# Order of the small matmuls in the state-space stage: pair by pair, or one 32-channel slice after the other

## The chip, the cores and the metric

The kernel runs on one core of one Trainium2 chip. The number that is compared is the device time of one execution in microseconds (us), median of three runs. A core has five engines that run their own instruction lists and meet through semaphores: PE (TensorE, matmuls), DVE (VectorE), ACT (ScalarE), POOL (GpSimd) and SP (which here only issues the loads of the weights).

## The reference, cut to what matters

Two layers of a hybrid attention block are followed by one block whose second half of channels goes through a complex diagonal state-space model. Only that part is touched:

```
bu_re = einsum('blgc,gnc->blgn', u32, bb_re)      # 64 groups of 16 channels, 64 states each
bu_im = einsum('blgc,gnc->blgn', u32, bb_im)
_, _, s_re, s_im = lax.associative_scan(_scan_combine, (a_re_t, a_im_t, bu_re, bu_im), axis=1)
y = (einsum('blgn,gcn->blgc', s_re, c_re) - einsum('blgn,gcn->blgc', s_im, c_im)
     + d_skip.reshape(N_SSM_GROUPS, SSM_GROUP) * u32)
g = gelu(y)
```

The sequence has 512 tokens. The kernel takes them two at a time, so that a scan runs over 256 chunks (`CHUNKS`); for the two tokens of a chunk there are separate small matrices.

## The kernel before, in words

Everything that is large is a product of activations [128 x 512] with weights that are streamed from HBM in units of 4 x 256 columns. ACT rounds a unit to `w_hi` (line 532), POOL makes the rest `w_lo` (line 519), and PE multiplies three times (lines 1658 to 1660): 24 matmuls of 512 columns a unit. ACT may round a unit only when PE has finished the unit four places before it, since there are four slots. SP orders the loads in the order of the units.

The state-space stage has 16 steps (`STEPS`). Step m works on 64 channels, as two slices of 32 channels (half `h` = 0 and 1), each with 128 states:

- `inputs_step(m)` on PE: for each half and for the real and the imaginary part `r`, two float32 matmuls with 32 rows of weights and 128 columns of weights, [32*128] in the trace, over 256 chunks. The results stand in `s_ps` (m even) or `t_ps` (m odd, which the trace calls to_ps). They are counted on `bu_done`.
- `state_step(m)` on DVE: rotates them by an angle (lines 1456 to 1464), scans them (line 1471), rotates back (lines 1477 to 1486) and writes `s_re` and `s_im`. Line 1477 may overwrite `s_re` only when PE has used the states of the step before (`ssm_y`).
- `outputs_step(m)` on PE: for each half one matmul with 32 rows and 32 columns of weights ([32*32], line 2044) and four with 128 rows and 32 columns ([128*32], lines 2046 to 2052) into `o_ps`. They are counted on `ssm_y`.
- `gelu(k)` on DVE (lines 1493 to 1496) after every second step, then a tanh on ACT (line 770), then `gelu_end(k)` (line 1501).
- `trig(m + 1)` on ACT (lines 765 and 766) makes the sine and cosine of the next step from angles that DVE makes (lines 1433 to 1445).

The order is written out by hand. PE's list has 16 rounds. Round m has one or two units of gate weights (one in rounds 4, 8 and 12, two in the other rounds from 1 to 15), `inputs_step(m + 1)` behind the first of them, and `outputs_step(m - 1)` at the end. DVE's list for round m is `angles(m + 1)`, in every second round `gelu` and `gelu_end`, and `state_step(m)`. ACT's list for round m is the rounding of the units up to four places beyond those of round m, in some rounds a copy of gate values (line 779), `trig(m + 1)`, and in every second round the tanh. After the last step ACT issues the transfer that brings all gates back (line 805, att<-gate_scratch); DVE scales them (line 1559) and goes on.

A row tile or column tile below means that a matmul takes only 32 or 64 of the 128 rows or columns of PE's array, by the partitions of its operands; two such matmuls can use different parts of the array.

Of the kernel before, what the change touches and what calls it, by code (L numbers as in the profile page):

```python
# [178 lines left out]
def build_program(nc, x, positions, w_in, w_uq, w_ukv, w_out, p_2, w_in_2, w_pool_2, w_glu_2, w_out_2, w_ple_2,  # L179
                  w_ple_gate_2, params, ssm_params, consts, out):  # L180
    at, UNITS, ROUNDS = plan_units()
    with ExitStack() as ctx:
# [341 lines left out]
        def _(act):  # L524
# [279 lines left out]
            act.wait_ge(ssm_y, 2 * STEPS)  # L804
# [91 lines left out]
        def _(dve):  # L896
# [550 lines left out]
            def state_step(n):  # L1447
# [7 lines left out]
                dve.wait_ge(bu_done, 2 * n + 2)  # L1455
# [18 lines left out]
                if n:  # L1474
                    dve.wait_ge(ssm_y, 2 * n)
# [13 lines left out]
            def gelu(k):  # L1489

                y = tiles[:, 8 + k]
                dve.wait_ge(ssm_y, 4 * k + 4)
                own.link(stt(y, y, C("dskip", k), o_ps[:, k % 2, :], ALU.mult, ALU.add))
                own.link(tt(tmp_s, y, y, ALU.mult))
                own.link(ts(tmp_s, tmp_s, 0.044715, 1.0, ALU.mult, ALU.add))
                tt(tmp_s, tmp_s, y, ALU.mult).then_inc(gelu_in, 1)
# [155 lines left out]
        def _(pe):  # L1652
# [356 lines left out]
            def inputs_step(m):  # L2009
# [10 lines left out]
                chs = [slice(32 * q, 32 * q + 32) for q in (2 * (m % 2), 2 * (m % 2) + 1)]  # L2020
                for r in range(2):
                    ps = [(s_ps, t_ps)[m % 2][:, h, r * CHUNKS:(r + 1) * CHUNKS] for h in range(2)]
                    for h, ch in enumerate(chs):
                        pe.matmul(ps[h], b_st[ch, k, r], x_k[ch, 1], start=True, stop=False)
                    for h, ch in enumerate(chs):
                        mm = pe.matmul(ps[h], ab_st[ch, k, r], x_k[ch, 0], start=False, stop=True)
                        if r == 1:
                            mm.then_inc(bu_done, 1)

            def outputs_step(m):  # L2030
# [6 lines left out]
                half = []  # L2037
                for h in range(2):
# [3 lines left out]
                    half.append((ch, y, s_re[:, h * CHUNKS:(h + 1) * CHUNKS], s_im[:, h * CHUNKS:(h + 1) * CHUNKS]))  # L2042
                for ch, y, re, im in half:
                    pe.matmul(y[:, 0], cb_st[ch, k], x_k[ch, 0], start=True, stop=False)
                for ch, y, re, im in half:
                    pe.matmul(y[:, 0, 1:CHUNKS], ca_st[:, k, 0, ch], re[:, 0:CHUNKS - 1], start=False, stop=False)
                for ch, y, re, im in half:
                    pe.matmul(y[:, 0, 1:CHUNKS], ca_st[:, k, 1, ch], im[:, 0:CHUNKS - 1], start=False, stop=True)
                for ch, y, re, im in half:
                    pe.matmul(y[:, 1], c_st[:, k, 0, ch], re, start=True, stop=False)  # L2050
                for ch, y, re, im in half:
                    pe.matmul(y[:, 1], c_st[:, k, 1, ch], im, start=False, stop=True).then_inc(ssm_y, 1)
# [89 lines left out]
```

## Time and profile before

| | |
|---|---|
| three runs | 2863.05, 2867.89 and 2873.32 us, median 2867.89 us |
| the profiled execution | 2867.89 us, span of its trace 2866.1 us, granted PE clock 0.967 on average |
| PE busy | 2679.4 us (93%) |
| DVE busy | 1517.8 us (53%), in the state-space stage nearly all the time |
| ACT, POOL busy | 887.3 us (31%), 1195.9 us (42%) |
| state-space stage | 1949 to 2261 us of the span |

Busy shares are of the whole span. In a timeline each row is a group of like instructions that follow each other on one engine; in brackets stands how long the engine had been idle before it, and what ended that. A float32 matmul of the touched kind leaves two rows of records in the trace (two passes), so x4 stands for two matmuls.

### The profile page before, as it was taken

To read this page: it belongs to the slowest core of one execution; us is meant where nothing else is said; L and a number is where in the kernel's file an instruction comes from. 1 tells how busy PE (TensorE), PEld (TensorE's weight loads), DVE (VectorE), ACT (ScalarE), POOL (GpSimd) and SP (SyncE) were. 2 spreads that over 40 slices of the span, in tenths; PEclk is the share of its full clock that TensorE was granted. 3 is DMA by queue.
4 is the path that set the end of the run, shared out by engine and by line. 5 is a ranking of instruction groups with operands and counts; after the bars stand their busy time and mean duration, and the time that the engine had idled before them with its cause. 6 is when DMAs were issued, how large, how long until landed. Compare 5 with 4: busy or idle time off the path is not lost. (4 is left out here: it accounts for less than half of the span.)

```text
span 2866.1 us, 34963 instructions
## 1 busy us (share of the span) xinstructions
PE 2679.4 (93%) x12638; PEld 2124.9 (74%) x12638; DVE 1517.8 (53%) x2088; ACT 887.3 (31%) x1802; POOL 1195.9 (42%) x860
## 2 busy tenths in 40 slices
PE   7999999999998999999999999788888989999996
PEld 5777877877786787887787788576555667788885
DVE  3553137468535654216548832848999684311524
ACT  4233214226323332323324522412222232322321
POOL 5452442442443653343352254433322354455551
PEclk9999999999999999999999999899888999999998
DMA  4332332321432433232232333332112323433331
GB/s 156 96 111 73 95 88 59 88 74 52 169 96 73 140 96 96 78 98 75 62 93 59 115 124 99 104 110 81 58 61 66 120 79 88 151 99 96 103 95 73
DMA packets 246198, 268.67 MB, mean 94 GB/s; under 512 B 20544, under 2 KB 237248, under 8 KB 243648
## 3 DMA queue, kind: packets, MB, share of 16 engines
q1 hardware_dynamic: 240512, 222.33, 26.2%
q10 hardware_dynamic: 5568, 44.74, 4.0%
q8 instruction: 78, 1.28, 0.2%
q14 instruction: 40, 0.33, 0.0%
HBM read 246.06 MB, written 20.97 MB: 93 GB/s over the span
## 5 line engine op out<-in xcount | busy, mean ns | idle before, releaser
L519 POOL TENSOR_TENSOR w_lo<-w_raw,w_hi 128x512 fp32r<-128x512 f32 x856 | 1195.7, 1420 | 1626.4 <-ACT w_hi L532 1626.2
L1658 PE MATMUL gemm_ps<-act_hi,w_hi 128*128 128x512 f32 x2848 | 1141.4, 401 | 77.5 <-DVE tiles L909 23.1
L1659 PE MATMUL gemm_ps<-act_lo,w_hi 128*128 128x512 f32 x2848 | 1117.2, 392 | 0.0
L1660 PE MATMUL gemm_ps<-act_hi,w_lo 128*128 128x512 f32 x2848 | 1117.1, 392 | 0.0
L532 ACT CAST w_hi<-w_raw 128x512 fp32r<-128x512 f32 x856 | 486.4, 618 | 1440.2 <-PE gemm_ps L1660 1249.5
L1658 PEld LDWEIGHTS gemm_ps<-act_hi,w_hi 128*128 128x128 f32 x2848 | 540.0, 190 | 226.0 <-issue 92.3
L1660 PEld LDWEIGHTS gemm_ps<-act_hi,w_lo 128*128 128x128 f32 x2848 | 539.4, 189 | 115.6
L1659 PEld LDWEIGHTS gemm_ps<-act_lo,w_hi 128*128 128x128 f32 x2848 | 540.5, 190 | 112.3 <-issue 4.3
L909 DVE TENSOR_TENSOR tiles<-gemm_ps,rstd 128x512 f32<-128x512 f32 (+1 forms) x58 | 39.3, 688 | 286.4 <-PE gemm_ps L1660 281.7
L1316 DVE COPY tiles<-gemm_ps 128x512 f32 x32 | 22.2, 692 | 210.0 <-PE gemm_ps L1660 209.5
L1609 DVE TENSOR_TENSOR tiles<-gemm_ps,att 128x512 f32<-128x512 f32 x16 | 11.0, 690 | 141.6 <-PE gemm_ps L1660 141.6
L985 DVE TENSOR_TENSOR att<-to_ps,sin_t 128x512 f32<-128x512 f32 x40 | 27.6, 689 | 88.9 <-PE to_ps L1755 88.9
L1023 DVE TENSOR_REDUCE small<-s_ps 128x1 f32<-128x128 f32 (+5 forms) x48 | 26.7, 557 | 82.3 <-PE s_ps L1799 81.9
L1639 DVE SCALAR_TENSOR_TENSOR att<-att 128x512 f32 x16 | 12.7, 793 | 104.0 <-ACT att L886 90.0
L1814 PE MATMUL to_ps<-cst,att 128*128 128x128 f32 x384 | 58.5, 275 | 7.0 <-ACT att L607 4.6
L585 ACT ACTIVATE att<-att,small 128x256 f32<-128x256 f32 (+1 forms) x128 | 60.1, 473 | 15.0 <-DVE small L1019 14.2
L917 DVE SCALAR_TENSOR_TENSOR act_lo<-tiles,col,act_hi 128x512 fp32r<-128x512 f32 x48 | 48.7, 1028 | 23.7 <-ACT act_hi L658 23.1
L1814 PEld LDWEIGHTS to_ps<-cst,att 128*128 128x128 f32 x384 | 47.2, 141 | 18.4 <-issue 5.5
L996 DVE TENSOR_TENSOR tiles<-tiles,att 128x512 f32<-128x512 f32 x36 | 56.1, 1559 | 1.2
L1658 PE MATMUL gemm_ps<-sub_hi,w_hi 128*128 128x512 f32 x96 | 42.1, 439 | 14.2 <-DVE tiles L1508 13.9
L1471 DVE TENSOR_TENSOR_SCAN att<-scol,att 128x256 f32<-128x256 f32 x64 | 53.8, 900 | 0.0
L592 ACT ACTIVATE att<-s_ps,small 128x128 f32<-128x128 f32 (+1 forms) x64 | 31.8, 500 | 70.7 <-DVE small L1024 70.7
(380 smaller groups left out, 3039.0 us busy)
## 6 DMA issues: line engine op xcount, KB each, us to landing
w_raw<-in_w_in_dram SPq DMA_DIRECT2D x248, 512.0 KB
w_raw<-in_w_out_dram SPq DMA_DIRECT2D x96, 512.0 KB
w_raw<-in_w_ple_gate_dram SPq DMA_DIRECT2D x32, 512.0 KB
gate_scratch<-att ACTq DMA_DIRECT2D x16, 512.0 KB, 2.7
x_scratch<-tiles ACTq DMA_DIRECT2D x4, 2048.0 KB, 8.0
att<-x_scratch ACTq DMA_DIRECT2D x2, 4096.0 KB, 12.4
w_raw<-in_w_glu_dram SPq DMA_DIRECT2D x32, 256.0 KB
tiles<-in_x_dram ACTq DMA_DIRECT2D x4, 1024.0 KB, 10.6
```

What stands on the lines that cost most here:

```text
L519: ins = pool.tensor_tensor(w_lo[:, s, k], w_raw[:, s, k], w_hi[:, s, k].bitcast(F32), ALU.subtract)
L532: act.copy(w_hi[:, slot, k:k + 2], w_raw[:, slot, k:k + 2]).then_inc(whi_done, 1)
L585: act.activation(v, v, ACT.Exp, bias=sm[:, 4 + j:5 + j], scale=SCALE[br], accum_out=sm[:, 8 + j:9 + j])
L592: last = act.activation(prob[n % 3][:, c * 512:c * 512 + nk], src, ACT.Exp, bias=sm[:, 4 + c:5 + c], scale=SCALE[br], accum_out=sm[:, 8 + ...
L909: tt(dst, ps[:, f, :], scale[:], ALU.mult).then_inc(bank_taken[f], 1)
L917: ins = stt(act_lo[:, kt], tiles[:, kt], scale, act_hi[:, kt].bitcast(F32), ALU.mult, ALU.subtract)
L996: tt(t, t, sq[:, n % 2], ALU.add).then_inc(roped, 1)
L1471: m_z = own.mark(dve.tensor_tensor_scan(z[:, v], mag, z[:, v], 0.0, ALU.mult, ALU.add))
L1658: pe.matmul(ps, left_hi, right_hi, start=first, stop=False, skip_group_check=True)
L1659: pe.matmul(ps, left_hi, right_lo, start=False, stop=False, skip_group_check=True)
L1660: return pe.matmul(ps, left_lo, right_hi, start=False, stop=last, skip_group_check=True)
L1814: mm = pe.transpose(t_ps[:, a, k * 128:(k + 1) * 128], prob[n % 3][:, a * 512 + k * 128:a * 512 + (k + 1) * 128], ident)
```

## The change

Both PE functions are written half after half in place of pair by pair. Before, each kind of matmul was issued for half 0 and at once for half 1, which lie in other rows (`inputs_step`) or other columns (`outputs_step`) of the array. After it, all matmuls of half 0 stand first and then all of half 1. Each step is counted once on `bu_done` and on `ssm_y` (before: once for each half), and the waits on DVE and ACT are halved to match. The matmuls, their operands and their number are the same, as are the lists of all other engines.

```diff
@@ DVE and ACT: the counts
-            act.wait_ge(ssm_y, 2 * STEPS)
+            act.wait_ge(ssm_y, STEPS)
-                dve.wait_ge(bu_done, 2 * n + 2)
+                dve.wait_ge(bu_done, n + 1)
-                    dve.wait_ge(ssm_y, 2 * n)
+                    dve.wait_ge(ssm_y, n)
-                dve.wait_ge(ssm_y, 4 * k + 4)
+                dve.wait_ge(ssm_y, 2 * k + 2)
@@ PE: inputs_step
-                chs = [slice(32 * q, 32 * q + 32) for q in (2 * (m % 2), 2 * (m % 2) + 1)]
-                for r in range(2):
-                    ps = [(s_ps, t_ps)[m % 2][:, h, r * CHUNKS:(r + 1) * CHUNKS] for h in range(2)]
-                    for h, ch in enumerate(chs):
-                        pe.matmul(ps[h], b_st[ch, k, r], x_k[ch, 1], start=True, stop=False)
-                    for h, ch in enumerate(chs):
-                        mm = pe.matmul(ps[h], ab_st[ch, k, r], x_k[ch, 0], start=False, stop=True)
-                        if r == 1:
-                            mm.then_inc(bu_done, 1)
+                for h in range(2):
+                    q = 2 * (m % 2) + h
+                    ch = slice(32 * q, 32 * q + 32)
+                    for r in range(2):
+                        ps = (s_ps, t_ps)[m % 2][:, h, r * CHUNKS:(r + 1) * CHUNKS]
+                        pe.matmul(ps, b_st[ch, k, r], x_k[ch, 1], start=True, stop=False)
+                        mm = pe.matmul(ps, ab_st[ch, k, r], x_k[ch, 0], start=False, stop=True)
+                mm.then_inc(bu_done, 1)
@@ PE: outputs_step
-                for ch, y, re, im in half:
                     pe.matmul(y[:, 0], cb_st[ch, k], x_k[ch, 0], start=True, stop=False)
-                for ch, y, re, im in half:
                     pe.matmul(y[:, 0, 1:CHUNKS], ca_st[:, k, 0, ch], re[:, 0:CHUNKS - 1], start=False, stop=False)
-                for ch, y, re, im in half:
                     pe.matmul(y[:, 0, 1:CHUNKS], ca_st[:, k, 1, ch], im[:, 0:CHUNKS - 1], start=False, stop=True)
-                for ch, y, re, im in half:
                     pe.matmul(y[:, 1], c_st[:, k, 0, ch], re, start=True, stop=False)
-                for ch, y, re, im in half:
-                    pe.matmul(y[:, 1], c_st[:, k, 1, ch], im, start=False, stop=True).then_inc(ssm_y, 1)
+                    mm = pe.matmul(y[:, 1], c_st[:, k, 1, ch], im, start=False, stop=True)
+                mm.then_inc(ssm_y, 1)
```

PE's list at `inputs_step(2)`, before the change; x2 are half 0 and half 1:

```order
L2024 MATMUL s_ps<-tiles,att 128x256 x2
L2026 MATMUL s_ps<-tiles 128x256 x2
L2024 MATMUL s_ps<-tiles,att 128x256 x2
L2026 MATMUL s_ps<-tiles 128x256 x2
L1658 MATMUL gemm_ps<-act_hi,w_hi 128x512
```

The same place in the changed kernel:

```order
L2025 MATMUL s_ps<-tiles,att 128x256
L2026 MATMUL s_ps<-tiles 128x256
L2025 MATMUL s_ps<-tiles,att 128x256
L2026 MATMUL s_ps<-tiles 128x256
L2025 MATMUL s_ps<-tiles,att 128x256
L2026 MATMUL s_ps<-tiles 128x256
L2025 MATMUL s_ps<-tiles,att 128x256
L2026 MATMUL s_ps<-tiles 128x256
```

The first four of these rows are half 0 and the last four half 1, so the first matmul of half 1 moved from the second to the fifth place.

PE's list at `outputs_step(0)`, before the change, again x2 for the two halves:

```order
L2044 MATMUL to_ps<-tiles,cst 32x256 x2
L2046 MATMUL to_ps<-att,tiles 32x255 x2
L2048 MATMUL to_ps<-att,tiles 32x255 x2
L2050 MATMUL to_ps<-att 32x256 x2
L2052 MATMUL to_ps<-att 32x256 x2
```

And in the changed kernel:

```order
L2041 MATMUL to_ps<-tiles,cst 32x256
L2042 MATMUL to_ps<-att,tiles 32x255
L2043 MATMUL to_ps<-att,tiles 32x255
L2044 MATMUL to_ps<-att 32x256
L2045 MATMUL to_ps<-att 32x256
L2041 MATMUL to_ps<-tiles,cst 32x256
L2042 MATMUL to_ps<-att,tiles 32x255
L2043 MATMUL to_ps<-att,tiles 32x255
L2044 MATMUL to_ps<-att 32x256
L2045 MATMUL to_ps<-att 32x256
```

Five matmuls of half 0 now stand ahead of the five of half 1, and the list goes from the [32*32] kind to the [128*32] kind twice in a step, and once back.

## Rows read from the trace of the kernel before

**Rows 1.** Windows: us, busy time of each engine, granted clock, DMA share, GB/s.

```profile
1949.09:2260.97 311.88, 264.59 (x1297) 184.03 (x1297) 293.67 (x516) 86.52 (x136) 105.02 (x68) 0.87 0.22 71
2017.48:2091.90 74.42, 63.85 (x315) 43.94 (x313) 71.96 (x131) 21.20 (x33) 21.78 (x16) 0.86 0.20 64
```

**Rows 2.** Waits, 1949 to 2262: who waited for whom, us in total, times, longest.

```profile
PE to_ps L2044 <- DVEq L1487: 21.8, 4, 5.8
PE to_ps L2024 <- DVE att L1464: 16.0, 6, 4.1
DVE tiles L1501 <- ACT att L770: 9.4, 7, 5.2
```

**Rows 3.** Timeline of PE at an inputs step: start us, us, engine, line, operation.

```profile
1968.21 0.72 PE L2024 MATMUL to_ps<-tiles,att 32*128 32x256 f32 x4
...
1970.22 0.50 PE L1658 MATMUL gemm_ps<-act_hi,w_hi 128*128 128x512 f32 x1
```

**Rows 4.** Timeline of PE at the first outputs step.

```profile
1983.23 0.39 PE L1660 MATMUL gemm_ps<-act_hi,w_lo 128*128 128x512 f32 x1
1983.55 0.64 PE L2044 MATMUL to_ps<-tiles,cst 32*32 32x256 f32 x4
1984.12 0.62 PE L2046 MATMUL to_ps<-att,tiles 128*32 128x255 f32 x4
...
1985.97 0.50 PE L1658 MATMUL gemm_ps<-act_hi,w_hi 128*128 128x512 f32 x1
```

**Rows 5.** Timeline of PE at three other places: whole array, row tiles, column tiles.

```profile
401.68 1.02 PE L1755 MATMUL to_ps<-tiles,cst 128*128 128x512 f32 x2
...
653.81 1.14 PE L1781 MATMUL s_ps<-att,tiles 64*128 64x256 f32 x8
...
1932.31 1.48 PE L2001 MATMUL to_ps<-att,tiles 128*32 128x32 f32 x128
```

**Rows 6.** Timeline, first DVE use of s_re after outputs steps 0 and 1; end of the second.

```profile
1988.99 0.66 DVE L1477 TENSOR_TENSOR att<-att,cos_t 128x512 f32<-128x512 f32 x1
...
2001.72 0.50 PE L1658 MATMUL gemm_ps<-act_hi,w_hi 128*128 128x512 f32 x1
...
2004.96 0.66 DVE L1477 TENSOR_TENSOR att<-att 128x512 f32<-128x512 f32 x1
```

**Rows 7.** Timeline of ACT in rounds 3, 5 and 13.

```profile
2015.22 1.14 ACT L532 CAST w_hi<-w_raw 128x512 fp32r<-128x512 f32 x2 [6.53 <-PE gemm_ps L1660]
...
2019.50 0.63 ACT L770 ACTIVATE att<-att 128x512 f32<-128x512 f32 x1 [0.70 <-DVE att L1496]
...
2053.08 0.63 ACT L765 ACTIVATE att<-att 128x512 f32<-128x512 f32 x1 [1.80 <-DVE att L1445]
...
2056.95 0.63 ACT L770 ACTIVATE att<-att 128x512 f32<-128x512 f32 x1 [1.33 <-DVE att L1496]
...
2202.28 0.63 ACT L765 ACTIVATE att<-att 128x512 f32<-128x512 f32 x1 [0.45 <-DVE att L1445]
...
2206.08 0.63 ACT L770 ACTIVATE att<-att 128x512 f32<-128x512 f32 x1 [1.25 <-DVE att L1496]
```

**Rows 8.** Timeline of PE at outputs step 3 and inputs step 7, both after a wait.

```profile
2032.30 1.06 PE L2044 MATMUL to_ps<-tiles,cst 32*32 32x256 f32 x4 [4.96 <-DVEq L1487]
...
2036.64 0.50 PE L1658 MATMUL gemm_ps<-act_hi,w_hi 128*128 128x512 f32 x1
...
2062.19 1.22 PE L2024 MATMUL to_ps<-tiles,att 32*128 32x256 f32 x4 [4.07 <-DVE att L1464]
...
2065.91 0.79 PE L1658 MATMUL gemm_ps<-act_hi,w_hi 128*128 128x512 f32 x1
```

**Rows 9.** Timeline at the last outputs step and behind it.

```profile
2256.28 1.06 PE L2044 MATMUL to_ps<-tiles,cst 32*32 32x256 f32 x4 [5.82 <-DVEq L1487]
...
2260.97 0.75 DVE L1493 SCALAR_TENSOR_TENSOR tiles<-tiles,col,to_ps 128x512 f32<-128x512 f32 x1 [4.80 <-PE to_ps L2052]
...
2301.06 0.79 PE L1658 MATMUL gemm_ps<-act_hi,w_hi 128*128 128x512 f32 x1 [6.92 <-DVE tiles L909]
```

More of the change, by code:

```diff
@@ L2036, in outputs_step @@
                 x_k = tiles[:, 8 + k, :].rearrange("p (j e) -> p e j", e=2)
-                half = []
                 for h in range(2):
@@ L2041, in outputs_step @@
                     y = o_ps[ch, k % 2, :].rearrange("p (j e) -> p e j", e=2)
-                    half.append((ch, y, s_re[:, h * CHUNKS:(h + 1) * CHUNKS], s_im[:, h * CHUNKS:(h + 1) * CHUNKS]))
-                for ch, y, re, im in half:
+                    re, im = (v[:, h * CHUNKS:(h + 1) * CHUNKS] for v in (s_re, s_im))
                     pe.matmul(y[:, 0], cb_st[ch, k], x_k[ch, 0], start=True, stop=False)
-                for ch, y, re, im in half:
                     pe.matmul(y[:, 0, 1:CHUNKS], ca_st[:, k, 0, ch], re[:, 0:CHUNKS - 1], start=False, stop=False)
-                for ch, y, re, im in half:
                     pe.matmul(y[:, 0, 1:CHUNKS], ca_st[:, k, 1, ch], im[:, 0:CHUNKS - 1], start=False, stop=True)
-                for ch, y, re, im in half:
                     pe.matmul(y[:, 1], c_st[:, k, 0, ch], re, start=True, stop=False)
-                for ch, y, re, im in half:
-                    pe.matmul(y[:, 1], c_st[:, k, 1, ch], im, start=False, stop=True).then_inc(ssm_y, 1)
+                    mm = pe.matmul(y[:, 1], c_st[:, k, 1, ch], im, start=False, stop=True)
+                mm.then_inc(ssm_y, 1)
             inputs_step(0)
```

## Prediction

> **What bounds the kernel now.** The page's first part has PE busy for nearly the whole span, so at first sight any time added to PE is added to the end. Windows of the state-space stage say something else. There DVE is busy 293.67 of 311.88 us and PE 264.59, at a mean granted clock of 0.87 [rows 1]. The waits confirm it: in this stage PE waits for DVE ten times, 37.8 us in all (four times before an outputs step, six times before an inputs step), while DVE waits for a tanh of ACT seven times, 9.4 us [rows 2], and for PE itself only at the end, 4.80 us [rows 9]. So the stage goes at DVE's pace, PE has slack in most of it, and the question is where PE's lateness reaches DVE. Behind the stage the chain is tight: the last outputs step releases a gelu on DVE (2260.97), that releases the return of the gates, which DVE needs, and at 2301.06 PE waits 6.92 us for DVE [rows 9]. What the last outputs step is late therefore arrives at the end in full, and PE's units between 2261 and 2301 do not hide it.
>
> **How wide the small matmuls run now.** A float32 matmul over the whole array with 512 columns takes two records; the group of two lasts 1.02 us of which the second record's own 0.59 is the last part, so one record is 0.43 and one of 256 columns 0.21 (estimate by columns) [rows 5]. An inputs step has 8 matmuls, 16 records: 16 x 0.21 = 3.4 us one after the other. It takes 1970.22 - 1968.21 = 2.01 us [rows 3]. The two halves run beside each other, eight slots of 0.22. An outputs step has 20 records, 4.3 us in a row, and takes 1985.97 - 1983.55 = 2.42 us [rows 4]. Again both halves share the slots.
>
> **Inputs steps after the change: I take 0.** The halves now stand four matmuls (eight records) apart. Does PE look that far ahead? Two places in the trace answer. In the sliding-window scores (line 1781) the code issues two matmuls of row tile 0 and then two of row tile 1, yet the eight records take 1.14 us including the 0.38 of the last, so four slots of about 0.2 rather than eight [rows 5]. In the setup at line 2001 each of four column tiles gets two matmuls in a row, and 128 records of 32 columns (0.027 each, 3.4 us in a row) are done in 1.48 us [rows 5]: tile 3 runs while tile 0 still has work, twelve records earlier. So in one tiling kind, PE starts a matmul of a free tile ahead of up to twelve older records; eight is inside that. Bounds: 0, and 3.62 - 1.81 = 1.8 us a step if the order were kept strictly (eight more slots of 0.226).
>
> **Outputs steps after the change: I take 2.42 us each.** Here the kind of tile changes inside the step. From the last record of a unit to the first [32*32] one is 1983.55 - 1983.23 = 0.32 us, where a slot is 0.22, and from [32*32] to [128*32] 0.57 us pass for two slots, while the four [128*32] groups of two slots take 1985.97 - 1984.12 = 1.85, 0.46 each with the last change in it [rows 4]. A change costs 0.1 us and seems to wait until the array is empty. With half 0 ending in [128*32] and half 1 beginning with [32*32], nothing of half 1 can start beside half 0 then: the step is its present length twice, +2.42 us. Bounds: 0, if PE starts half 1 early all the same, and 2.42.
>
> The Trainium skill, "TensorEngine Tiling (Array Packing)", section Key Properties, says that changing the tiling mode, as against the tile, drains TensorE; the extra 0.1 us of rows 4 agrees. By that rule the outputs steps double and the inputs steps, which stay in one mode, need not.
>
> The fewer semaphore counts are worth nothing: DVE waits only for the last one before as well. The other lists are the same.
>
> **The sum.** Sixteen outputs steps are 38.7 us more on PE, most of it in slack. I follow it in time.
>
> 1. Rounds 1 to 3. PE does not wait there at all. Outputs step 0 ends at 1985.97 and DVE needs it at 1988.99: 3.02 to spare, 2.42 used [rows 4, 6]. Outputs step 1 is 4.84 late at 2001.72, against 3.24 to spare (2004.96): DVE loses 1.6 [rows 6]. Then the units of round 3 are 4.84 late; ACT's rounding at 2015.22 waits for them, and the tanh behind it had only 0.70 to spare [rows 7]. So the tanh, gelu_end and the whole DVE list are 4.84 - 0.70 = 4.1 late, the 1.6 included. **+4.1**
> 2. Rounds 4, 8 and 12 have one unit and PE waits for DVE there (4.96 us before outputs step 3 [rows 8]), so PE starts these outputs steps in time with DVE again. But in rounds 5, 9 and 13 the same ACT chain has to bear the longer step. It has 1.80 + 1.33 = 3.1 to spare in round 5 and 0.45 + 1.25 = 1.7 in round 13 [rows 7]; for round 9 I take that of round 5. At full clock the step is 2.42 longer: 0, 0 and 0.7 late. But after the wait outputs step 3 ran at half clock, 2036.64 - 2032.30 = 4.34 us [rows 8], and by that it is 4.4 longer: 1.3, 1.3 and 2.7 late. The wait before it shrinks only to about 3.3 us: PE is idle 74.42 - 63.85 = 10.6 us in rounds 4 to 7 [rows 1], so 1.5 beside the waits of 4.96 and 4.07; 4.96 + 1.5, less three outputs steps = 7.3, plus DVE's 4.1. After a wait of 4.07 the clock also fell (inputs step 7 took 3.72 in place of 2.01 [rows 3, 8]). Between 0.7 and 5.3, I take the middle. **+3.0**
> 3. Rounds 6, 10 and 14. The wait before the inputs step, 4.07 in round 6 [rows 8], is eaten by two longer outputs steps (4.84). PE is 0.8 late, but the step then runs at full clock and gives back 1.7, and the unit behind it more. **0**
> 4. The last outputs step. PE waits 5.82 before it and it runs at half clock, 4.6 us from 2256.28 to the gelu [rows 9]. After the change it is 4.84 at full clock, 9.2 at half. Its wait is still over 3 us. Between +0.2 and +4.6, the middle. **+2.4**
>
> Together +9.5 us, of 5.0 to 14.0 with the bounds of terms 2 and 4. The profiled execution took 2867.89 us, 1.8 more than its span of 2866.1, and is the median of the three runs itself. So 2877.4 us, 2873 to 2882.
>
> **Rivals.**
>
> *Nothing is lost.* PE starts half 1 of an outputs step beside half 0 in spite of the change of kind, since other rows and columns of the array are free. Place: the sixteen outputs steps; price 0 in place of 2.42. The time begins to grow from 0.35 us a step on, half the 0.70 that the tanh of round 3 has to spare behind two of them [rows 7]. For it: line 2001, where PE looks twelve records ahead [rows 5], and outputs half 1 is only ten away. Against: the 0.1 us and the missing overlap at each change of kind [rows 4]. The time stays at 2868.
>
> *The order is strict everywhere.* Then an inputs step costs 1.8 more too, 4.24 us a round. Up to the tanh of round 3 there are two outputs and four inputs steps: 12.1 - 0.7 = +11.4. In the four rounds from 2017.48 to 2091.90 PE is idle 10.6 us [rows 1] and loses at least 3.6 to the half clock (4.34 - 2.42 and 3.72 - 2.01 [rows 3, 4, 8]) that it would get back; four rounds want 17.0, so PE is short by up to 2.8 a cycle of four rounds. With half of that three times it is +4.2. The last step +0.2 to +4.6. In all +18, 2886 us, 2880 to 2892. For it only that each tile's queue could be short; against it rows 5 speak plainly.
>
> The Trainium skill, "TensorE: Matmul & The Clock Gate", Part 3, states that matmuls start and end in strict program order and only weight loads are pulled ahead. By that rule it is this rival, and the time is 2886; the 1.14 us for eight records at line 1781 disagrees, so it gets no more than the chance below.
>
> *PE stays warm.* A busier PE might keep its clock and gain. The half clock costs PE at least 3.6 us in four rounds, but DVE sets the pace there, so the gain stays on PE. It is inside the ranges.
>
> **Chances.** Outputs doubled only: 0.55. Nothing lost: 0.22. All strict: 0.20. Anything else: 0.03. About 0.3% (8.6 us, 2859 to 2876) is what a measurement can tell from no change. Of the first case some six tenths lie above 2876.5, of the second nearly none, of the third all: slower 0.55, within 0.3% 0.42, faster 0.03. Range 2866 to 2889: it takes in the second case and about half of the third.
>
> **What would show it.** Right: an outputs step of 4.8 us at full clock with the groups of [32*32] records twice in it, x2 each; inputs steps still near 2.0 us; the tanh of round 3 some 4 us late; DVE waiting for line 770 in round 3 with 4 us more than 0.7; the last gelu behind a wait of 5 to 9 us. Wrong: an outputs step of 2.4 to 2.6 (nothing lost), an inputs step of 3.8 (all strict), or a stage that is longer by much more than the last step and the waits of DVE add up to.

## The result and the profile after

| | before | after |
|---|---|---|
| median, us | 2868.38 (4 runs, 2863.05 to 2873.32) | 2894.73 (4 runs, 2891.45 to 2896.6) |
| ratio | 1 | 1.0091 (95%: 1.007 to 1.0112) |
| profiled execution, its span | 2867.89, 2866.1 | 2892.7, 2890.9 |
| granted PE clock, whole span | 0.967 | 0.971 |
| an inputs step, full clock | 2.01 | 3.02 |
| an outputs step, full clock | 2.42 | 4.80 |

The change makes the kernel slower by 26.3 us (medians), where 9.5 had been forecast; its 2894.73 lies above the range of 2866 to 2889. The page of the changed kernel has 53.0 us more work on PE and 10.9 us less on DVE than the one before:

```profile
PE 2732.4 (95%) x12638; PEld 2152.3 (74%) x12638; DVE 1506.9 (52%) x2088; ACT 886.8 (31%) x1802; POOL 1200.6 (42%) x860
```

That is 16 x (1.01 + 2.38) = 54.2 us by the two steps, of which 24.8 came to the end. First the inputs step, which answers to [rows 3], as a timeline of PE (start in us, duration, line, operation):

```profile
1971.72 0.71 PE L2025 MATMUL to_ps<-tiles,att 32*128 32x256 f32 x2
1972.28 0.61 PE L2026 MATMUL to_ps<-tiles 32*128 32x256 f32 x2
1972.73 0.72 PE L2025 MATMUL to_ps<-tiles,att 32*128 32x256 f32 x4
1973.18 0.72 PE L2026 MATMUL to_ps<-tiles 32*128 32x256 f32 x4
1973.75 0.61 PE L2025 MATMUL to_ps<-tiles,att 32*128 32x256 f32 x2
1974.20 0.61 PE L2026 MATMUL to_ps<-tiles 32*128 32x256 f32 x2
1974.74 0.50 PE L1658 MATMUL gemm_ps<-act_hi,w_hi 128*128 128x512 f32 x1
```

The counts tell the halves apart: x2 is one half alone, x4 are both beside each other. Half 0 runs alone for two matmuls, then both halves, then half 1 alone for two. So 4 + 4 + 4 slots (a slot is the time of one record) stand where there were 8. Then the outputs step, which answers to [rows 4]:

```profile
1989.12 0.63 PE L2041 MATMUL to_ps<-tiles,cst 32*32 32x256 f32 x2
1989.69 0.62 PE L2042 MATMUL to_ps<-att,tiles 128*32 128x255 f32 x2
...
1991.53 0.63 PE L2041 MATMUL to_ps<-tiles,cst 32*32 32x256 f32 x2
1992.09 0.62 PE L2042 MATMUL to_ps<-att,tiles 128*32 128x255 f32 x2
...
1993.93 0.50 PE L1658 MATMUL gemm_ps<-act_hi,w_hi 128*128 128x512 f32 x1
```

The [32*32] group stands in it twice, never more than x2: nothing of half 1 ran beside half 0, and the 4.81 us are nearly twice the 2.42 of [rows 4].

Who waits now, in the state-space stage (which answers to [rows 2]); us in total, times, longest:

```profile
DVE tiles L1501 <- ACT att L770: 30.5, 7, 8.2
...
PE to_ps L2041 <- DVEq L1487: 12.1, 4, 3.6
...
DVE att L1477 <- PE to_ps L2045: 11.5, 2, 6.5
...
DVE tiles L1493 <- PE to_ps L2045: 5.0, 1, 5.0
```

DVE's waits rose from 14.2 us to 47.0, PE's for DVE fell from 37.8 to 12.1: both are late by turns. The timeline has them in order of time; the brackets are the idle time before and what ended it:

```profile
1994.04 0.69 DVE L1477 TENSOR_TENSOR att<-att,cos_t 128x512 f32<-128x512 f32 x1 [5.05 <-PE to_ps L2045]
...
2014.78 0.69 DVE L1477 TENSOR_TENSOR att<-att 128x512 f32<-128x512 f32 x1 [6.47 <-PE to_ps L2045]
...
2035.02 0.69 DVE L1501 SCALAR_TENSOR_TENSOR tiles<-att,tiles 128x512 f32<-128x512 f32 x1 [8.20 <-ACT att L770]
...
2047.75 1.06 PE L2041 MATMUL to_ps<-tiles,cst 32*32 32x256 f32 x2 [3.58 <-DVEq L1487]
...
2287.34 0.75 DVE L1493 SCALAR_TENSOR_TENSOR tiles<-tiles,col,to_ps 128x512 f32<-128x512 f32 x1 [5.03 <-PE to_ps L2045]
...
2327.55 0.80 PE L1658 MATMUL gemm_ps<-act_hi,w_hi 128*128 128x512 f32 x1 [7.38 <-DVE tiles L909]
```

Already in rounds 1 and 2 DVE waits for an outputs step, before the first late tanh. The last two rows answer to [rows 9]. What is late at the last gelu still arrives at the end in full: the time behind it was 605.1 us before, 603.6 after and 605.5 in e2. I measure the stage from the first instruction of DVE's state step 0 to the last gelu, and cut it at the beginnings of state steps 3 and 13. That gives the forecast's terms a measure each (us):

| part of the stage | before | more: forecast | more: after | more: e2 |
|---|---|---|---|---|
| rounds 1 to 3 | 62.7 | 4.1 | 11.8 | 4.6 |
| rounds 4 to 13 | 186.6 | 3.0 | 12.7 | 12.3 |
| from there to the last gelu | 53.5 | 2.4 | -1.2 | 4.1 |
| the stage | 302.8 | 9.5 | 23.3 | 21.0 |

The stage began 3.0 us later in the profiled execution of after (the code ahead of it is the same) and the rest behind it was 1.5 shorter; 23.3 + 3.0 - 1.5 = 24.8, the difference of the spans. e2 is the kernel with only the outputs steps changed, below: the very case that the forecast had worked out. Most of what it lost beyond the forecast is in the second row, 9.3 of 11.5 us.

### The profile page after: what moved, and what is told of

Its sections match the earlier page's. It is cut to its first block and busy times, and to the rows that moved or that the text cites. A ratio compares the mean times of both kernels' runs of the same rounds, so it can differ in the third digit from the quotient of the medians.

```text
span 2890.9 us, 34963 instructions
## 1 busy us (share of the span) xinstructions
PE 2732.4 (95%) x12638; PEld 2152.3 (74%) x12638; DVE 1506.9 (52%) x2088; ACT 886.8 (31%) x1802; POOL 1200.6 (42%) x860
## 5 line engine op out<-in xcount | busy, mean ns | idle before, releaser
L1639 DVE SCALAR_TENSOR_TENSOR att<-att 128x512 f32 x16 | 12.7, 793 | 104.0 <-ACT att L886 90.0
L585 ACT ACTIVATE att<-att,small 128x256 f32<-128x256 f32 (+1 forms) x128 | 60.1, 473 | 15.0 <-DVE small L1019 14.2
L1658 PE MATMUL gemm_ps<-sub_hi,w_hi 128*128 128x512 f32 x96 | 42.0, 437 | 14.2 <-DVE tiles L1508 13.9
L909 DVE TENSOR_TENSOR att<-gemm_ps,rstd 128x512 f32<-128x512 f32 x32 | 21.6, 687 | 56.5 <-PE gemm_ps L1660 56.2
## 6 DMA issues: line engine op xcount, KB each, us to landing
att<-x_scratch ACTq DMA_DIRECT2D x2, 4096.0 KB, 12.4
```

The lines of the kernel that those rows point to most:

```text
L585: act.activation(v, v, ACT.Exp, bias=sm[:, 4 + j:5 + j], scale=SCALE[br], accum_out=sm[:, 8 + j:9 + j])
L909: tt(dst, ps[:, f, :], scale[:], ALU.mult).then_inc(bank_taken[f], 1)
L1658: pe.matmul(ps, left_hi, right_hi, start=first, stop=False, skip_group_check=True)
```

## The experiments

All kernels were run beside the kernel before on the same chip (2865.7, 2864.53, 2865.07 and 2865.22 us in the four sets). IN and OUT are an inputs and an outputs step at full clock, from the profiled executions.

| kernel | median us (number of runs) | ratio, 95% | IN | OUT | stage |
|---|---|---|---|---|---|
| e1 inputs only | 2875.9 (6) | 1.0036 (1.0021 to 1.0052) | 3.02 | 2.42 | 316.9 |
| e2 outputs only | 2891.56 (4) | 1.0088 (1.0068 to 1.0108) | 2.01 | 4.80 | 323.8 |
| e3 inputs by two | 2868.56 (10) | 1.0012 (1.0001 to 1.0023) | 2.11 | 2.42 | 302.8 |
| e4 outputs, one kind | 2868.27 (10) | 1.0007 (0.9998 to 1.0017) | 2.01 | 3.30 | 305.5 |
| e5 kinds mixed | 2874.69 (9) | 1.0034 (1.0021 to 1.0047) | 2.01 | 3.51 | 309.4 |
| e6 inputs three and one | 2871.17 (1) | none | 2.56 | 2.42 | 304.8 |
| e7 after, tanh first | 2890.1 (4) | 1.0086 (1.0067 to 1.0106) | 3.02 | 4.80 | 326.3 |
| e8 before, last tanh first | 2858.27 (12) | 0.9976 (0.9965 to 0.9986) | 2.01 | 2.42 | 293.6 |
| e9 wide filler | 2876.87 (8) | 1.0043 (1.0031 to 1.0056) | 2.01 | 2.42, even steps 4.8 more | 308.6 |
| e10 narrow filler | 2880.52 (4) | 1.0051 (1.0036 to 1.0066) | 2.01 | 2.42, even steps 4.86 more | 316.0 |
| e11 IN of e1, OUT of e4 | 2879.22 (4) | 1.0043 (1.0028 to 1.0058) | 3.02 | 3.30 | 314.7 |
| e12 e8, last outputs step earlier | 2859.79 (11) | 0.998 (0.9971 to 0.9989) | 2.01 | 2.42 | 290.8 |
| e13 e2, waits filled | 2878.38 (4) | 1.0043 (1.0026 to 1.006) | 2.01 | 4.80 | 318.6 |
| e14 after, waits filled | 2887.77 (4) | 1.0076 (1.006 to 1.0093) | 3.02 | 4.80 | 323.4 |

### Each half of the change alone: e1 and e2

e1 has the changed inputs_step and the outputs_step of before, e2 the other way round.

> Only inputs_step is written half after half, outputs_step stays pair by pair. Both theories expect an inputs step of 3.0 us in place of 2.0 (the changed kernel has 3.02) and an outputs step of 2.4. Theory 1 (my sum for the outputs steps was right, and the rest of the +26 us comes from the inputs steps that I had at nothing): the inputs alone cost +12 to +17 us, 2880 to 2885. Theory 2 (the loop PE, ACT's rounding, tanh, DVE was filled up by both together, each alone finds slack): 16 us more on PE, of which rounds 1 to 3 let DVE feel about 3 to 4 us (four steps x 1.0 less 0.7), and the rest is slack: +3 to +5 us, 2871 to 2873.

> Only outputs_step is written half after half, inputs_step stays pair by pair. This is the case that the forecast described. Outputs step 4.8 us, inputs step 2.0. Theory 1 (the sum of the forecast holds for its own case): +9.5 us, 5 to 14, so 2873 to 2882. Theory 2 (the forecast also undercounted what the ACT chain behind the outputs steps does in rounds 5, 9 and 13 after the half clock): +14 to +20 us, 2882 to 2888, with waits of DVE for the tanh (gelu_end) of 3 us or more in rounds 5, 9 and 13.

Alone they cost 10.2 and 25.9 us. e1 lies between what its two theories had, e2 above both of its own. e2 alone refutes the forecast, since it is the forecast's own case and costs nearly three times its 9.5 us.

Together they cost 26.3, less than their sum. A slack that both had used would have made the two together dearer, so that is not the reason. By the parts of the stage, e1 and e2 add up in rounds 1 to 3 (6.6 + 4.6, and 11.8 in the changed kernel), but not in rounds 4 to 13 (6.1 + 12.3 against 12.7) or behind them (1.4 + 4.1 against -1.2). The traces show one thing that goes with it: PE's waits for DVE in the stage are 31.1 us in e1, 23.8 in e2 and 12.1 in the changed kernel, and the last outputs step, which ran at half clock in e1 and e2 (4.54 and 9.06 us), ran at full clock there (4.81).

### How far PE looks ahead: e3 and e6

e3 (each pair of a half together, the two halves in turn) and e6 (three matmuls of a half, then the fourth):

```diff
 e3  for r in range(2):
+        for h in range(2):                  # b_st and ab_st of one half together
+            pe.matmul(ps, b_st[ch, k, r], x_k[ch, 1], start=True, stop=False)
+            mm = pe.matmul(ps, ab_st[ch, k, r], x_k[ch, 0], start=False, stop=True)
 e6
+    for n0, n1 in ((0, 3), (3, 4)):         # matmuls n0 to n1 of a half
+        for h in range(2):
```

> Outputs as before. inputs_step issues two matmuls of half 0, two of half 1, then again two and two (four records of one tile in a row in place of two before and eight after). Theory Q (each tile takes up to four records, one running and three waiting, in program order, and PE goes on to the next tile only when the last has been taken): inputs step 2.0 us, time as before, 2868 within 0.2%. Rival S (overlap comes only where the halves alternate one by one, and the 1.0 us saved against a strict order in the changed kernel came from something else): 2.5 to 3.0 us, and +3 to +5 us.

> The kernel before with inputs_step in the order three matmuls of half 0, three of half 1, one and one (six records of a tile in a row). Theory Q (a tile takes four records, one running and three waiting, in program order): half 1 starts when the third record of half 0 starts; from there on the two lag by two records and the last two stand alone, ten slots of 0.225 and the ends: 2.5 us for the step at full clock. Rival (PE looks no further than the next tile's first matmul, or eight records): 2.0 or 3.0.

e3 costs 2.9 us, with an interval that just excludes no change. Timeline of PE at an inputs step of e3, two matmuls of a half in a row:

```profile
1972.61 0.73 PE L2025 MATMUL to_ps<-tiles,att 32*128 32x256 f32 x4
1973.16 0.62 PE L2026 MATMUL to_ps<-tiles 32*128 32x256 f32 x4
```

And the beginning of one of e6, three in a row:

```profile
1970.81 0.71 PE L2030 MATMUL to_ps<-tiles,att 32*128 32x256 f32 x2
1971.37 0.38 PE L2030 MATMUL to_ps<-tiles 32*128 32x256 f32 x1
1971.37 0.49 PE L2030 MATMUL to_ps<-tiles,att 32*128 32x256 f32 x1
```

With two in a row (four records) all rows are x4, both halves from the start. With three, two records of half 0 run alone, and half 1 (the third row, at 1971.37) starts with the third record of half 0. With four, in the changed kernel, it starts with the fifth: 1972.735 beside 1972.729. All of these fit one rule, inferred from these starts: records are given out in the order of the list; a tile takes four of them, one that runs and three that wait; and the first of the next tile starts as soon as the last of the tile before has been taken. That makes 8, 10 and 12 slots. With 0.226 us a slot and 0.2 for the two changes of kind around a step, 8 slots are the 2.01 of the kernel before, and e3, e6 and the changed kernel come to 2.01, 2.46 and 2.91; measured were 2.11, 2.56 and 3.02, each 0.1 more.

### The change of kind apart from the order: e4 and e5

```diff
 e4  for ch, y, re, im in half: pe.matmul(... cb_st ...)          # [32*32], both halves
     for ch, y, re, im in half: pe.matmul(... ca_st[..., 0] ...)  # [128*32] from here
-    for ch, y, re, im in half:    # three of these lines go: four matmuls of half 0,
-    for ch, y, re, im in half:    # then four of half 1
-    for ch, y, re, im in half:
 e5
-    for ch, y, re, im in half:    # between cb_st and ca_st[..., 0]: the kinds alternate
```

> Inputs as before. outputs_step issues the two [32*32] matmuls first, then the four [128*32] ones of half 0, then the four of half 1, so that the kind of tile changes as often as before, but eight records of one tile stand in a row. Theory Q with the drain at a change of kind: 2.42 + 4 x 0.215 = 3.3 us for the outputs step, and +3 to +5 us on the time. Rival (the doubling in the changed kernel came from the long rows and not from the change of kind): 2.42 + 8 x 0.215 = 4.1 us and more than half of the full loss.

> The kernel before, but outputs_step issues line 2044 and line 2046 of half 0, then both of half 1, and the rest pair by pair. No tile gets more than four records in a row, so by the queue alone nothing would be lost; the kind of tile changes two times more in a step. With the drain at each change: [32*32] 0.57, [128*32] 0.54, [32*32] 0.57, then two slots of half 1 and six shared ones, so 0.57 + 0.54 + 0.57 + 8 x 0.216 + 0.1 = 3.5 us for the step, +1.1. Without it 2.4. Time: 1.1 x 16 = 18 us more on PE, mostly in slack as with the one-kind order (0.9 a step, no change of the time that could be told): 2866 to 2873.

Timeline of PE at an outputs step of e4:

```profile
1987.17 0.64 PE L2044 MATMUL to_ps<-tiles,cst 32*32 32x256 f32 x4
1987.74 0.62 PE L2046 MATMUL to_ps<-att,tiles 128*32 128x255 f32 x2
1988.19 0.59 PE L2047 MATMUL to_ps<-att,tiles 128*32 128x255 f32 x2
1988.62 0.38 PE L2048 MATMUL to_ps<-att 128*32 128x256 f32 x1
1988.63 0.40 PE L2046 MATMUL to_ps<-att,tiles 128*32 128x255 f32 x1
```

And at one of e5:

```profile
1991.10 0.63 PE L2044 MATMUL to_ps<-tiles,cst 32*32 32x256 f32 x2
1991.66 0.62 PE L2045 MATMUL to_ps<-att,tiles 128*32 128x255 f32 x2
1992.21 0.63 PE L2044 MATMUL to_ps<-tiles,cst 32*32 32x256 f32 x2
```

In e4 half 1 (last row) starts with the fifth [128*32] record of half 0, as the rule of four says, and the step has 14 slots in place of 10: 3.30. In e5 each [32*32] pair runs alone, though the next [32*32] pair uses other columns, and nothing overlaps across a change of kind: 3.51. So of the 2.38 us that an outputs step grew, 0.88 is what the order costs without a second change of kind (e4), and the other 1.5 came with that change. e4 has 14 us more work on PE and its median is 2.6 us higher, with an interval that includes no change; e5 has 17 more and costs 10.2, above the 2866 to 2873 that were expected. What makes that difference isn't known.

e1, with 16 us more on PE, costs 10.2 too, and there the traces tell part of it. Up to the beginning of state step 3, e1 loses 6.6 us and e4 1.5. By count the tanh of round 3 stands behind four inputs steps but only two outputs steps: 4.0 - 0.7 = 3.3 against 1.8 - 0.7 = 1.1. And in e1 the clock stood at half in two stretches of 3.4 us, from 1972.60 and from 1982.84, with PE busy before and in them, which is another 3.4 us of PE's work; e4 has none there. The first of them (windows: us, busy time of PE, PEld, DVE, ACT, POOL, then the granted clock):

```profile
1972.60:1976.01 3.41, 3.41 (x9) 2.67 (x9) 3.41 (x5) 0.00 (x0) 1.48 (x1) 0.50 0.51 154
```

Later DVE's waits for the tanh of rounds 7 and 11 grew by 2.3 and 4.2 us in e1 and not at all in e4. Inputs steps 7, 11 and 15, at half clock behind a wait before (3.71 us), took 4.61, 5.00 and 5.59 in e1 and 2.01 in e4.

### Is it the tanh or PE: e7, e9 and e10

e7 is the changed kernel with ACT's tanh ahead of the round's other work. e9 and e10 are the kernel before with extra matmuls at the beginning of every even outputs step, wide (the whole array) or narrow ([128*32]); what they write, the step overwrites.

```diff
 e7 (ACT's list)
+    if m % 2 and m > 2:
+        split_until(u0 + units_by(m) - 1 + RING)
+        gelu((m - 3) // 2)        # was behind the rounding, the copy and trig
 e9 (outputs_step)
+    if m % 2 == 0:
+        for _ in range(21): pe.matmul(o_ps[:, k % 2, :], act_hi[:, 0, 0:128], act_hi[:, 1], ...)
 e10
+        for _ in range(11): pe.matmul(o_ps[0:32, k % 2, 0:CHUNKS], c_st[:, k, 0, 0:32], s_re[:, 0:CHUNKS], ...)
```

> The changed kernel, but in every second round ACT does the tanh of gelu before the rounding of the round's last unit and before the sine and cosine, so that gelu_end on DVE no longer stands behind PE's last unit of that round. Theory A (PE's lateness reaches DVE mainly through this chain, the seven waits at gelu_end of 1.7 to 8.2 us in the changed kernel): these waits fall to about 1 us, and 12 to 18 us of the 26 come back, 2877 to 2883. Theory B (PE, with its half clock, is the bound of the loop by itself): the waits move to the use of s_re or to inputs, and the time stays within 5 us of the changed kernel's, 2890 to 2895.

> The kernel before with both steps pair by pair, plus 21 extra full-array matmuls (fp32r, 512 columns, their result is overwritten and never read) ahead of every even outputs step: 21 x 0.227 = 4.8 us every second round, together 38 us on PE, as much as the outputs steps half after half add. Theory C (what hurts in the outputs-only kernel is to a large part that the array is used narrowly: the granted clock falls to half for 10 to 14 us a cycle and makes 4.8 us steps into 9.1): with wide work in place of narrow the clock stays up and the time is clearly below that kernel's 2891, at 2872 to 2880. Theory D (any 38 us on PE cost the same): 2887 to 2893.

> The counterpart of the wide filler: the kernel before, with 11 extra float32 matmuls of the narrow [128*32] kind (256 columns, 11 x 0.43 = 4.7 us, overwritten and never read) at the same places, ahead of every even outputs step. Same time on PE at full clock, same places, a quarter of the array. Theory C (narrow work lets the granted clock fall, and that is what fills the loop): 2884 to 2892, a stage from the first state step to the last gelu of 318 to 326 us against 308.6 with the wide filler, and more half clock in it than its 27 us. Theory D (only the PE time and its place count): as with the wide filler, 2872 to 2880.

Waits in the stage of e7; us in total, times, longest:

```profile
DVE att L1478 <- PE to_ps L2046: 38.2, 7, 7.7
...
PE gemm_ps L1659 <- ACT att L779: 12.8, 2, 8.1
DVE tiles L1494 <- PE to_ps L2046: 11.6, 1, 11.6
...
DVE tiles L1502 <- ACT att L770: 6.5, 7, 2.3
```

The waits for the tanh fell from 30.5 us to 6.5, and the time stayed (1.0086 against 1.0091, intervals that overlap). DVE now waits for PE instead, 49.8 us with the last gelu, and a new wait came: twice PE itself stands, 12.8 us, for a copy of ACT (line 779) that is now behind the tanh. So taking the tanh out of the rounding chain doesn't give the time back. Because of that new wait e7 shows neither that the chain costs nothing in the changed kernel nor that PE binds it.

e9 and e10 put 38 and 39 us more on PE, in steps that don't follow a wait. They cost 12.3 and 15.5 us (e10 lies just above the range of its theory D), and their intervals overlap: that narrow matmuls cost more than wide ones isn't shown. But e2 put the same 38 us on PE and cost 25.9, with an interval above both: the amount of PE's work alone doesn't set the loss.

### The steps behind a wait: e13 and e14

Ahead of outputs steps 3, 7 and 11 PE waits for DVE: 4.60, 4.19 and 4.14 us in e2, 3.58 each time in the changed kernel. In both the clock stood at half (1.2 GHz) when the step began. The steps took 9.07, 9.06 and 9.06 us in e2, and 9.07, 9.06 and 6.46 in the changed kernel, where the clock rose again within the last of them. e13 is e2, and e14 the changed kernel, with wide matmuls in that waiting time, which adds 12.4 and 9.7 us of work (3 x 18 and 3 x 14 of 0.23 us).

```diff
 outputs_step, ahead of pe.wait_ge(state_done, m + 1)
+    if m in (3, 7, 11):
+        pe.wait_ge(gelu_in, k)
+        for _ in range(18):     # e14: 14
+            pe.matmul(o_ps[:, (k + 1) % 2, :], act_hi[:, 0, 0:128], act_hi[:, 1], ...)
```

> The outputs-only kernel, and 18 extra full-array matmuls (4.1 us, overwritten and never read) in PE's waits of 4.1 to 4.6 us ahead of outputs steps 3, 7 and 11. PE gets 12 us more work and no step of the kernel starts earlier. Theory H (term 2 of the forecast failed because in rounds 4, 8 and 12 PE's wait drops the clock to half, and the doubled step and the unit behind it then run slow, 9.07 us and 1.0 more, late for the tanh of rounds 5, 9 and 13): these steps take 4.8 us, the waits of DVE at gelu_end of rounds 5, 9 and 13 (4.0, 3.9 and 5.2 us) fall under 1 us, the stage from 323.8 to 311 to 315 us, the time to 2879 to 2883. Theory P (PE's work alone decides, wherever the clock stands): 12 us more of it cannot help, 2890 to 2896.

> The changed kernel with 14 such matmuls (3.2 us) in its waits of 3.58 us ahead of outputs steps 3, 7 and 11. Theory H: steps 3, 7 and 11 take 4.8 in place of 9.07, 9.06 and 6.46 us, the waits at gelu_end of rounds 5 and 9 fall from 4.9 and 4.7 to about 1 us, the stage from 326.1 to 314 to 318, the time to 2882 to 2886. Theory B (with both parts PE is the bound already, and the stretches at half clock without any wait decide): 2890 to 2896.

e2, timelines of PE at outputs step 3, of ACT's rounding behind it, and of DVE's wait for the tanh:

```profile
2039.88 1.06 PE L2042 MATMUL to_ps<-tiles,cst 32*32 32x256 f32 x2 [4.60 <-DVEq L1487]
...
2044.42 1.06 PE L2042 MATMUL to_ps<-tiles,cst 32*32 32x256 f32 x2
...
2062.93 1.14 ACT L532 CAST w_hi<-w_raw 128x512 fp32r<-128x512 f32 x2 [6.53 <-PE gemm_ps L1660]
...
2067.19 0.69 DVE L1501 SCALAR_TENSOR_TENSOR tiles<-att,tiles 128x512 f32<-128x512 f32 x1 [4.04 <-ACT att L770]
```

The same rounding in the kernel before (the step there starts at 2032.30 [rows 8]):

```profile
2050.14 1.14 ACT L532 CAST w_hi<-w_raw 128x512 fp32r<-128x512 f32 x2 [6.54 <-PE gemm_ps L1660]
```

And e13 at the same place, filler and step:

```profile
2036.74 4.37 PE L2036 MATMUL to_ps<-act_hi 128*128 128x512 f32 x18
...
2041.44 0.63 PE L2046 MATMUL to_ps<-tiles,cst 32*32 32x256 f32 x2 [0.33 <-DVEq L1487]
```

Windows of e2 over its stretch at half clock, us, busy time of PE, PEld, DVE, ACT, POOL, then the granted clock:

```profile
2036.30:2049.95 13.65, 10.06 (x22) 3.67 (x23) 13.45 (x28) 2.14 (x3) 1.12 (x1) 0.50 0.22 77
```

And of e13 over the same stretch:

```profile
2036.00:2050.00 14.00, 13.68 (x62) 8.62 (x59) 13.80 (x27) 3.53 (x6) 2.98 (x2) 1.00 0.22 75
```

In e2 the step began after 4.60 us of waiting, at half clock, and half 1 began 4.54 us after half 0; the whole step took 9.07. In e13 the clock stayed at 1.00, the three steps took 4.81, 4.81 and 4.80, and DVE's waits for the tanh in rounds 5, 9 and 13 went from 4.04, 3.85 and 5.22 to 0.70, 1.74 and 3.03. The kernel is 13 us faster than e2 with more work in it; the two intervals, 1.0068 to 1.0108 and 1.0026 to 1.006, don't overlap. That filling these three waits takes away about half of e2's loss is therefore shown. That it does so through the clock is what the trace says of the three steps. The size can't be followed in it: the profiled execution of e13 was its slowest, 2888.8 (the other three took 2876.78 to 2879.73), and in it the stage is only 5.2 us shorter than in e2 and two of the three waits are longer than the 1 us that was expected.

In the changed kernel the same filling gave 1.0076 against 1.0091, overlapping, so no difference is shown; 2887.77 lies between the ranges of its two theories. There the waits were shorter and one more thing was different. Two of its stretches at half clock, where PE hadn't been idle before:

```profile
2002.94:2006.35 3.41, 3.41 (x9) 2.63 (x8) 3.38 (x6) 0.00 (x0) 1.69 (x2) 0.51 0.41 154
2023.42:2026.83 3.41, 3.41 (x9) 2.74 (x9) 3.29 (x4) 0.00 (x0) 2.39 (x2) 0.51 0.02 5
```

PE was busy throughout (3.41 of 3.41). Both stretches begin at the end of an inputs step with its narrow matmuls, at 2002.62 and 2023.38; e14 has the same two. PE waits for DVE 4.7 us in e14's stage of 323.4, 12.1 of 326.1 in the changed kernel and 37.8 of 302.8 in the kernel before. That suggests that PE binds most of the changed kernel's stage, but no run shows it: in e14 the filler itself takes up waiting time, and DVE still waits 38.5 us.

### The change without its extra changes of kind: e11

e11 is e1's inputs step with e4's outputs step.

> Inputs half after half as in the changed kernel, outputs in the one-kind order (both [32*32] first, then half after half), so the change without its extra changes of kind. Inputs step 3.0, outputs step 3.3. PE gets 1.0 + 0.9 more a round, 30 us, against 54 in the changed kernel. If the costs of the two parts simply add: 14.1 + 2.7 = 17 us longer stage, 2882. If the loop first has to be full: 10 to 14 us, 2875 to 2879. If PE is the bound from here on: 20 us or more, 2885.

It costs 14.2 us, about e1 and e4 added (10.2 + 2.6), and 2879.22 is at the edge of the second range. Its interval overlaps that of e1, so the second part isn't told apart.

### A faster kernel: e8 and e12

```diff
 e8 (ACT's list of before, as e7 but for the last round alone)
+    if m == STEPS - 1:
+        split_until(u0 + units_by(m) - 1 + RING)
+        gelu((m - 3) // 2)
 e12 = e8 and (PE's list, behind the rounds)
     one_pair(("pi", 0), 0, 0)
-    one_pair(("pi", 0), 0, 1)
     outputs_step(STEPS - 1)
+    one_pair(("pi", 0), 0, 1)
```

> The kernel before, with the ACT order of the run above in the last round (15) alone. Theory A: gelu_end of round 15 waits 5.2 us there because the tanh stands behind PE's last gate unit; it falls to 0.7, DVE's last step ends 4.5 us earlier, PE has no wait of 5.8 us and no half clock before the last outputs step (2.4 in place of 4.6 us): 5 to 7 us less, 2859 to 2861. Rival: the scans and the gates behind it wait for something else (DMA, POOL sharing DVE's port) and nothing is gained.

> The kernel with the tanh ahead in the last round (it beats the one before by 0.24%), and the last outputs step ahead of the second unit of pool weights. There the last gelu still waits 5.29 us for PE, which does that unit (5.7 us) first. Theory A (the chain gelu, transfer of the gates, DVE is the critical one and PE has 6.9 us of waiting at its end to spare): about 2.5 us less than that kernel, 2854 to 2857. Rival (the unit moved behind then makes PE late by as much, or the wait drops PE to half clock): no change, 2857 to 2860.

DVE in e8, its wait for the tanh in round 15 (5.2 before, the longest of [rows 2]) and the last gelu:

```profile
2238.76 0.69 DVE L1504 SCALAR_TENSOR_TENSOR tiles<-att,tiles 128x512 f32<-128x512 f32 x1 [0.70 <-ACT att L770]
...
2254.53 0.75 DVE L1496 SCALAR_TENSOR_TENSOR tiles<-tiles,col,to_ps 128x512 f32<-128x512 f32 x1 [5.29 <-PE to_ps L2055]
```

DVE in e12, the last gelu and the gelu_end behind it:

```profile
2252.42 0.75 DVE L1496 SCALAR_TENSOR_TENSOR tiles<-tiles,col,to_ps 128x512 f32<-128x512 f32 x1 [2.67 <-PE to_ps L2055]
...
2259.81 0.83 DVE L1504 SCALAR_TENSOR_TENSOR tiles<-att,tiles 128x512 f32<-128x512 f32 x1 [4.72 <-ACT att L770]
```

e8 is the fastest kernel of this study, 6.3 us below the one before. The tanh no longer stands behind the roundings; DVE comes 4.5 us sooner there, and PE doesn't wait before the last outputs step, which runs at full clock (2.41 in place of 4.55). e12 shortens the last gelu's wait by 2.6 us more and gets nothing for it: at once behind it DVE waits 4.72 us for the tanh, 0.70 in e8. The wait has moved to ACT.

## Why the prediction was wrong, step by step

- **What bounds the kernel before: right in kind.** PE has slack there: e4 puts 14 us more on it for 2.6, e9 38 us for 12.3. The place where lateness arrives in full was also right: the time behind the last gelu hardly differs (605.1, 603.6 and 605.5 us in the kernel before, the changed one and e2).
- **Outputs steps, +2.42 each: right.** 4.80 measured (+2.38), with the [32*32] group twice. By the rule of the Trainium skill, "TensorEngine Tiling (Array Packing)", Key Properties, that a change of tiling mode drains the array, e5 should show lone [32*32] pairs, and it does.
- **Inputs steps, 0: wrong, the first step that failed.** Each is 1.0 us longer. I read "twelve records ahead" at line 2001 [rows 5] as one window over all tiles. But there each of the four tiles had only four records in a row, and at line 1781 also four. By e3, e6 and the changed kernel the bound is four for each tile, and a half of the changed step has eight in a row. Both rows fit that rule; I didn't ask how many of the records ahead belonged to one tile, though I had named a short queue for each tile as the one thing in favour of the strict order.
- **The order of starts.** The Trainium skill, "TensorE: Matmul & The Clock Gate", Part 3, says that matmuls start in strict program order. By that rule an inputs step would have come to about 3.8 us; it took 3.02, and half 1 started with half 0's fifth record, ahead of three older ones. For records of different tiles the measurement decides against it, as far as a queue of four reaches.
- **Term 1, +4.1: right for its own case, 4.6 in e2.** In the changed kernel it is 11.8. The inputs steps, four of them up to the tanh of round 3, add 4.0 by count; the other 3 us or so fit the two stretches of 3.4 us at half clock (2002.94 and 2023.42, above) where PE had not waited, which nothing in the forecast had. e1 comes out the same way, with two such stretches: 4.0 - 0.7 + 3.4 = 6.7, and 6.6 measured.
- **Term 2, +3.0: the term that was mis-sized, 12.3 in e2.** The chain was right, PE's unit, rounding, tanh, gelu_end in rounds 5, 9 and 13, and its waits are there. Two things were missing. I took the middle between full and half clock, 3.0, though [rows 8] showed 4.34 us for the step after that very wait: it ran at half clock for all of its 9.07 us. And I left out the unit behind: the rounding came 2062.93 - 2039.88 = 23.05 us after the step's beginning, in place of 2050.14 - 2032.30 = 17.84, so 5.2 later, where the step alone gives 4.7. Counted so for all three rounds (5.2, 4.7 and 4.4 later, less the spare of 3.1, 2.8 and 1.7), the tanh comes 2.1, 1.9 and 2.7 us late, 6.7 together. Measured from the beginning of the outputs step, gelu_end came 2.0, 1.8 and 3.1 later than before. DVE's waits in these rounds grew by more, 11.0 us, because DVE's own work ahead of each wait was 1.3 to 1.4 us shorter than before. It was as much longer elsewhere in rounds 4 to 13, and 1.3 more (busy 181.8 us against 180.4), which makes up the 12.3.
- **Term 3, 0: right for e2**, where inputs steps 7, 11 and 15 no longer wait and run at 2.01. In the changed kernel they run at full clock too, but DVE's waits for the tanh of rounds 7 and 11 grew from 0.7 to 1.7 and 4.3 us. The forecast had no term for these two.
- **Term 4, +2.4 of 0.2 to 4.6: 4.1 in e2**, at half clock for 9.06 us behind a wait of 4.56, near the upper bound. In the changed kernel it was -1.2: PE waited only 1.41 and ran that step at full clock (4.81, before 4.55 at half). I had said that its wait would still be over 3 us.
- **Terms that were added up: wrong.** They were taken one after the other, each with the waits and the clock of the kernel before. But what one part adds changes the waits, and with them the clock, of the next: e1 and e2 cost 10.2 and 25.9 alone and 26.3 together.
- **The rivals.** What came, outputs steps doubled and inputs steps half-way, was none of the three cases and had a chance of 0.03. "Nothing is lost" is refuted by 4.80. "The order is strict everywhere" had the nearest time, 2886 (2880 to 2892), for a wrong reason: 1.8 a step, where 1.0 came. "PE stays warm" holds in so far as PE's clock in the stage rose (0.88 to 0.93), and the time rose all the same.

What stays open: why e5 costs 10 us and e4 under 3 for much the same amount of PE's work (17 and 14 us); what makes DVE's own work shorter in some rounds and longer in others; how much of the changed kernel's loss is the clock that falls without a wait; and whether PE binds the changed kernel.

## What to carry to other kernels

Order small matmuls so that neighbours in the list are of the same tile kind and of different tiles. Two float32 matmuls of one tile in a row (four records) cost next to nothing here (0.1 us a step), each further one its own time. An engine's waiting time in a stage is no measure of what can be added to it: with 37.8 us of waits, 38 us more cost 12.3 us where they stood apart from the waits (e9) and 25.9 where part of them stood behind (e2). Price a step behind a wait at half clock, with the unit behind it. A late result that one engine hands to the next is often cured in a third engine's list: moving one tanh ahead (e8) gave 6.3 us, and no order of the matmuls that was tried gave any.

## What the runs showed of the hardware that was not expected

- **A tile takes four records.** IN of 2.01, 2.11, 2.56 and 3.02 us for one, two, three and four matmuls of a half in a row, and the first of half 1 beside the first, first, third and fifth record of half 0.
- **The clock falls without idle time.** In the changed kernel it was 0.51 from 2002.94 and from 2023.42, in e1 0.50 from 1972.60 and from 1982.84, with PE busy before and in all of these stretches. All four begin within 0.3 us of the end of an inputs step written half after half.
- **DVE runs slower beside POOL.** In e2 DVE's line 1479 once took 1.77 us, at the same step of the kernel before 0.68. In both kernels every execution of this line that POOL's work overlapped in full took 1.76 to 1.77 us, and every one apart from POOL 0.68 to 0.69. First the two rows of e2:

```profile
2074.10 3.39 POOL L519 TENSOR_TENSOR w_lo<-w_raw,w_hi 128x512 fp32r<-128x512 f32 x2 [7.97 <-ACT w_hi L532]
...
2074.57 1.77 DVE L1479 TENSOR_TENSOR att<-att,cos_t 128x512 f32<-128x512 f32 x1
```

and DVE in the kernel before, while POOL was idle:

```profile
2064.99 0.68 DVE L1479 TENSOR_TENSOR att<-att,cos_t 128x512 f32<-128x512 f32 x1
```

The Trainium skill, "GPSIMD Engine Reference", Specifications, says that GpSimd shares its SBUF interfaces with VectorE and contends with instructions of two SBUF inputs; the trace agrees. A shift of a few us between the lists can thus change DVE's own work: over the stage it is 284.6 us in the kernel before, 275.1 in the changed one and 290.9 in e10. That this is why is not shown by a run of its own.
